# Two transformer blocks in one launch: the loads of the modulation weights and the first block's norms in another order

## What is computed

```python
cond = jax.nn.silu(c)                                   # c: (1, 1024)
mod = (cond @ ada_w[l] + ada_b[l])[:, None, :]          # ada_w: 1024 x 6144
sh1, sc1, g1, sh2, sc2, g2 = jnp.split(mod, 6, axis=-1)
h = rms_norm(x, ln1_g[l]) * (1.0 + sc1) + sh1
x = x + g1 * hybrid_mixer(h, w_in[l], w_out[l], ...)    # w_in: 1024 x 2840
h = rms_norm(x, ln2_g[l]) * (1.0 + sc2) + sh2
x = x + g2 * sparse_moe(h, ...)
```

## Time and profile before

| | |
|---|---|
| median of 3 runs | 2072.49 us (2072.33 to 2079.0) |
| the profiled execution, first to last instruction | 2071.6 us |
| PE busy | 1912.6 us (92%) |
| DVE busy | 498.4 us (24%) |
| ACT busy | 288.5 us (14%) |
| DMA | 547.34 MB, mean 264 GB/s |
| chain that ended last | PE 71%, DMA 22%, DVE 4%, ACT 2% |

### The profile page before, as it was taken

The page is one execution under the profiler, slowest core; times in us unless marked ns, Lnnn a source line. Parts: engine busy times, 40 slices in busy tenths (PEclk is TensorE's granted clock), DMA queues, the critical chain, the costliest instruction groups (busy, mean ns, idle before and its releaser), DMA issues.

```text
span 2071.6 us, 21989 instructions
## 1 busy us (share of the span) xinstructions
PE 1912.6 (92%) x8646; PEld 1104.0 (53%) x8647; DVE 498.4 (24%) x1026; ACT 288.5 (14%) x560; POOL 83.7 (4%) x115
## 2 busy tenths in 40 slices
PE   5987889999999999999999998989999989799997
PEld 2444733333333333333333335867788868678886
DVE  1236232212222222222212223132110015511001
ACT  1025101001110011001101101043110010311000
POOL 4003500000000000000000001000000001000000
PEclk9999889999999999999999999999999999899999
DMA  9682449969999999999999995311343433333430
GB/s 352 250 257 85 180 193 418 417 244 401 419 417 417 418 418 417 417 419 417 417 418 419 417 417 213 130 73 41 122 144 141 144 120 118 114 117 139 163 122 21
DMA packets 133761, 547.34 MB, mean 264 GB/s; under 512 B 5874, under 2 KB 9154, under 8 KB 97778
## 3 DMA queue, kind: packets, MB, share of 16 engines
q1 hardware_dynamic: 131536, 544.33, 66.8%
q10 hardware_dynamic: 2178, 2.34, 0.4%
HBM read 545.60 MB, written 1.05 MB: 264 GB/s over the span
## 4 chain that ended last, share of the span: by engine, by line
PE 71%; DMA 22%; DVE 4%; ACT 2%; issue 1%; SPq 0%; ACTq 0%; POOL 0%; DVEq 0%
PE ps L997 21%; DMA ring<-in_exp_w 20%; PE ps L949 14%; PE ps L1091 11%; PE ps L974 6%; PE ps L692 4%; PE ps L921 3%; PE ps L905 2%; PE ps L852 1%; PE ps L642 1%; DMA ring<-in_ada_w 1%; ACT arena L1145 1%; PE ps L1041 1%; PE ps L652 1%; PE ps L780 0%
## 5 line engine op out<-in xcount | busy, mean ns | idle before, releaser
L949 PE MATMUL ps<-ring,arena 128*64 128x512 f32 x2112 | 465.0, 595 | 13.7 <-DMA ring<-in_exp_w 13.7
L997 PE MATMUL ps<-hn,ring 128*128 128x272 f32 (+1 forms) x1792 | 415.4, 395 | 27.0 <-DVE hn L1679 16.0
L997 PEld LDWEIGHTS ps<-hn,ring 128*128 128x128 f32 x1792 | 346.0, 194 | 96.3 <-issue 23.4
L949 PEld LDWEIGHTS ps<-ring,arena 128*64 128x64 f32 x2112 | 155.8, 138 | 304.2 <-issue 266.8
L974 PE MATMUL ps<-arena 128*64 128x512 f32 x1056 | 233.9, 595 | 36.9 <-ACT arena L1145 36.9
L1091 PE MATMUL ps<-arena,ring 128*128 128x272 f32 (+1 forms) x1024 | 228.4, 386 | 1.0 <-ACT arena L1328 1.0
L1091 PEld LDWEIGHTS ps<-arena,ring 128*128 128x128 f32 x1024 | 194.4, 190 | 34.9 <-ACT arena L1328 1.8
L974 PEld LDWEIGHTS ps<-arena 128*64 128x64 f32 x1056 | 75.4, 137 | 174.2 <-issue 174.2
L1145 ACT ACTIVATE arena<-ps 128x512 f32<-128x512 f32 (+3 forms) x171 | 90.9, 536 | 373.4 <-PE ps L974 239.5
L921 PE MATMUL ps<-arena 128*128 128x512 f32 x272 | 132.4, 618 | 0.8 <-ACT arena L1145 0.8
L1626 DVE TENSOR_SCALAR arena<-arena 128x64 f32<-128x64 f32 x68 | 14.2, 251 | 391.4 <-PE ps L949 391.4
(11 more groups left out here) (341 smaller groups left out, 1201.9 us busy)
## 6 DMA issues: line engine op xcount, KB each, us to landing
ring<-in_exp_w SPq DMA_DIRECT2D x128, 2048.0 KB, 22.6
arena<-in_exp_w SPq DMA_DIRECT2D x64, 2048.0 KB, 19.6
ring<-in_mlp_w_up SPq DMA_DIRECT2D x16, 2048.0 KB, 7.6
ring<-in_mlp_w_down SPq DMA_DIRECT2D x16, 2048.0 KB, 7.7
ring<-in_ada_w SPq DMA_DIRECT2D x12, 2048.0 KB, 12.9
ring<-in_sb_w_qkv SPq DMA_DIRECT2D x6, 2048.0 KB, 14.4
ring<-in_w_in SPq DMA_DIRECT2D x5, 2048.0 KB, 9.9
ring<-in_lru_w_in SPq DMA_DIRECT2D x4, 2048.0 KB, 7.9
```

The lines of the kernel that those rows point to most:

```text
L949: last = mm(bank(2 + part)[64 * h:64 * h + 64, :], lhs, w[:, k % 2, at:at + 512], start=False, stop=(k == C - 1))
L997: last = mm(bank((n0 + q) % 8)[:, lo:TT], w[:, k, P * q:P * q + P], act[:, k, lo:TT], start=(k == 0), stop=(k == C - 1))
```

## The change

`A_LOADS` now brings group 0, all six chunks of `w_in`, the compressed layer's weights, and only then the eight loads of groups 1 and 2. SP no longer waits for the parameters. PE's modulation parts go from the projections to the compressed keys: group 1's four parts behind the hidden layer, group 2's four behind the compressed scores. `modulated_norm` is cut in three: `normed` (reciprocal and `x * rstd`), `affine`, and `modulated` (`* affine + shift` in one pass). For the first norm `normed` stands ahead of `modulation(0)`.

```diff
-A_LOADS = ([("ada", 0, k) for k in range(4)]
-           + [load for c in range(6) for load in (("in", 0, c), ("ada", 1 + c // 4, c % 4))]
-           + [("cmp", 0, 0), ("ada", 2, 2), ("ada", 2, 3)] + [("wout", 0, h) for h in range(2)])
+A_LOADS = ([("ada", 0, k) for k in range(4)] + [("in", 0, c) for c in range(6)] + [("cmp", 0, 0)]
+           + [("ada", 1 + k // 4, k % 4) for k in range(8)] + [("wout", 0, h) for h in range(2)])
...
-    sp.wait_ge(s["p0_loaded"], 16 * len(PARAMS[0]))
     for n, load_of in enumerate(A_LOADS):
...
         last.then_inc(s["z_done"], 1)
-        if t == 1:
-            if v == 1:
-                pe.wait_ge(s["root_ready"], 1)
-            modulation_part(1 + c // 4, c % 4)
...
     last.then_inc(s["cmp_hidden"], 1)
-    modulation_part(2, 2)
-    turn_modulation(1)
+    for k in range(4):
+        modulation_part(1, k)
     pe.wait_ge(s["cmp_gelu"], 1)
...
     last.then_inc(s["cmp_kv_done"], 1)
-    modulation_part(2, 3)
-    turn_modulation(2)
+    turn_modulation(1)
     pe.wait_ge(s["cmp_k_ready"], 1)
...
     last.then_inc(s["cmp_scored"], 1)
+    for k in range(4):
+        modulation_part(2, k)
+    turn_modulation(2)
...
-    def modulated_norm(number, gain, scale, shift):
-        link(v.scalar_tensor_tensor(m.affine[:], m.modT[:, scale:scale + C], 1.0, col(gain, C), ALU.add, ALU.mult))
+    def normed(number):
         dve.wait_ge(s["root_ready"], number)
         link(v.reciprocal(m.rstd[:, 0:T], m.root[:, 0:T]))
         first = chain.n
         for c in range(C):
-            v.scalar_tensor_tensor(m.hn[:, c, META:TT], m.xT[:, c, META:TT], m.affine[:, c:c + 1],
-                                   m.rstd[:, 0:T], ALU.mult, ALU.mult).then_inc(s["dve_chain"], 1)
+            v.tensor_tensor(m.hn[:, c, META:TT], m.xT[:, c, META:TT], m.rstd[:, 0:T],
+                            ALU.mult).then_inc(s["dve_chain"], 1)
         chain.n += C
+        return first
+    def affine(gain, scale):
+        link(v.scalar_tensor_tensor(m.affine[:], m.modT[:, scale:scale + C], 1.0, col(gain, C), ALU.add, ALU.mult))
+    def modulated(shift, first):
         for c in range(C):
             dve.wait_ge(s["dve_chain"], first + c + 1)
-            v.tensor_scalar(m.hn[:, c, META:TT], m.hn[:, c, META:TT], m.modT[:, shift + c:shift + c + 1],
-                            None, ALU.add).then_inc(s["h_ready"], 1)
+            v.tensor_scalar(m.hn[:, c, META:TT], m.hn[:, c, META:TT], m.affine[:, c:c + 1],
+                            m.modT[:, shift + c:shift + c + 1], ALU.mult, ALU.add).then_inc(s["h_ready"], 1)
...
-    modulation(0)
     dve.wait_ge(s["x_placed"], 4)
-    modulated_norm(1, PC_LN1, M_SC1, M_SH1)
+    made = normed(1)
+    modulation(0)
+    affine(PC_LN1, M_SC1)
+    modulated(M_SH1, made)
...
-    modulated_norm(2, PC_LN2, M_SC2, M_SH2)
+    affine(PC_LN2, M_SC2)
+    modulated(M_SH2, normed(2))
```

More of the change, by code:

```diff
@@ L1400, in modulated_norm @@
         for c in range(C):
-            v.scalar_tensor_tensor(m.hn[:, c, META:TT], m.xT[:, c, META:TT], m.affine[:, c:c + 1],
-                                   m.rstd[:, 0:T], ALU.mult, ALU.mult).then_inc(s["dve_chain"], 1)
+            v.tensor_tensor(m.hn[:, c, META:TT], m.xT[:, c, META:TT], m.rstd[:, 0:T],
+                            ALU.mult).then_inc(s["dve_chain"], 1)
         chain.n += C
+        return first
+    def affine(gain, scale):
+        link(v.scalar_tensor_tensor(m.affine[:], m.modT[:, scale:scale + C], 1.0, col(gain, C), ALU.add, ALU.mult))
+    def modulated(shift, first):
         for c in range(C):
             dve.wait_ge(s["dve_chain"], first + c + 1)
-            v.tensor_scalar(m.hn[:, c, META:TT], m.hn[:, c, META:TT], m.modT[:, shift + c:shift + c + 1],
-                            None, ALU.add).then_inc(s["h_ready"], 1)
+            v.tensor_scalar(m.hn[:, c, META:TT], m.hn[:, c, META:TT], m.affine[:, c:c + 1],
+                            m.modT[:, shift + c:shift + c + 1], ALU.mult, ALU.add).then_inc(s["h_ready"], 1)
+    dve.wait_ge(s["x_placed"], 4)
+    made = normed(1)
     modulation(0)
-    dve.wait_ge(s["x_placed"], 4)
-    modulated_norm(1, PC_LN1, M_SC1, M_SH1)
+    affine(PC_LN1, M_SC1)
+    modulated(M_SH1, made)
     dve.wait_ge(s["x_turned"], 5)
@@ L1472, in program_vector @@
     v.tensor_scalar(m.hid, m.hid2, 0.5, None, ALU.mult).then_inc(s["cmp_gelu"], 1)
-    modulation(1)
     dve.wait_ge(s["cmp_hidT_done"], 1)
@@ L1485, in program_vector @@
     v.tensor_copy(m.kcn[0:64, 0, :], m.kcn[0:64, 1, :]).then_inc(s["cmp_k_ready"], 1)
-    modulation(2)
+    modulation(1)
     dve.wait_ge(s["cmp_kT_done"], 1)
@@ L1511, in program_vector @@
                     ALU.mult).then_inc(s["cmp_probs"], 1)
+    modulation(2)
     for u in range(UNITS + 2):
```

## The result

| | before | after |
|---|---|---|
| median in the comparison (5 runs each) | 2076.01 us (2072.33 to 2079.0) | 2086.91 us (2082.97 to 2091.13) |
| ratio, 95% interval | 1 | 1.0055 (1.0038 to 1.0073) |
| the profiled execution | 2071.6 us | 2085.2 us |

The change makes the kernel slower by 0.55%. 3.5 of these are the kernel before itself, which ran at 2076.0 in the comparison and not at 2072.5; the other 11.8 are the change.

A forecast was written before the change was run, and what follows sets the result against it. It took a chain of waits to bound the kernel: group 0's loads, then PE up to attention. On the profiled span -6.0 - 3.05 - 10.4 + 19.6 - 0.8 - 0.2 = -0.9; median 2071.6 us, range 2066 to 2079.

The forecast's parts named there:

- The step that failed: At the start: ACT free at 12.1 us, before the parameters' turns, so its DMA issuing costs nothing; squares' sum ends at 24.3.
- the start: Up to the first projection matmul: without SP's wait and with the norm split, projections begin at 34.5 instead of 40.5, -6.0 us.
- The parameters: At the start: `x` shares DMA engines with group 0's loads and lands at 11.3, parameter set 0 at 14.5 us.
- The first rival: Start lost to its own transfers: parameters at about 20 us, projections at 40.5 and low clock; 2080.7 us, slower; 13%.
- The clock at the projections: First two projection half-chunks on PE run at 2.4 GHz after a shorter idle gap: -3.05 us (bounds -3.05 and 0).
- The parts: Projections on PE: six modulation parts of 1.85 us leave, five gained whole and 1.2 from the sixth: -10.4 us.
- The compressed keys: Hidden layer's end to attention: group 2's late loads land last, attention starts 32.2 us after instead of 12.6: +19.6 us.
- The fourth rival: Before attention: last loads land while small steps run, so they don't end last; attention at T + 20 (T: hidden layer's end), 2060 us; 4%.
- The attention's clock: Attention's first unit, held up about 1.6 us by the 1.2 GHz level; half of it gained, -0.8 us.
- The second norm: Second norm's products and adds on DVE: cheaper product, only first multiply-and-add ahead of the router matmuls: -0.2 us.
- Behind 277 us: From pass 0 to the end: the earlier difference is carried along whole, no further change.

The follow-up runs named there:

- the last experiment: Kernel before with the norm cut, `router_w` issued last of ACT's small loads and SP waiting only for `c`: 2068.4 us, 0.9968 of the kernel before.

## Why the prediction was wrong, point by point

**The step that failed** is "ACT was free at 12.1, before that, so its DMA issuing hides nothing and costs nothing", with its bound "if the longer backlog held its last two issues for up to 3 us". The issue behind `router_w` was held for 13.9 us, to 24.0, 7 past the parameters' landing. E, the end of the squares' sum, was 34.34 and not 24.3. Of these 10.0, 2.7 are the parameters (17.2 for 14.5), 6.75 the hold (E is 27.59 with `router_w` last; PE's sums took 5.85 in the kernel after and 5.52 in that one), 0.6 the rest. Another 0.9 came from the first `w_in` chunk, which landed E + 11.1 instead of E + 10.2, 9.12 after its issue (7.8). Sum 10.9, the whole miss at the start. The warning stood in the timeline of the kernel before, 0 to 25 us:

```profile
9.83 1.53 ACTq L1164 DMA_DIRECT2D rb<-in_router_b  x1
```

That is two to five times its neighbours' 0.3 to 0.7, at a moment when `x` had landed and group 0 had just begun. I had looked at when ACT was free and not at which issue had made it late.

**The parameters.** The sum was `x` alone 5.2, plus 16 packets in turn with q1's (4.7), plus 3.4. The turns came as said (626 packets to 621). What was missing is that `x` did not begin: from its issue at 1.44 to 5 us q1 moved 119 packets, seven an engine, and of `x` nothing. It landed at 13.84 instead of 11.3, and the parameters took the 3.4 behind it that I had given them. The later start in the last experiment takes this away.

**The first rival**, a start lost to its own transfers, was given 13% and 2080.7 us, and is nearest to what came. Its condition, parameters at about 20 us, did not hold (17.2), and neither did its price: with the parameters at 17.04 and ACT free, the projections start at 38.5, still 2 us before the old 40.51. Its direction was right and its mechanism is the smaller part. The rule behind it (the Trainium skill, "DMA: Bandwidth & Descriptors", section "Queues, rings and completion order": an engine drains a whole packet of some 9 to 17 descriptors before it turns to the next queue) is not what this case shows, and the measurement decides. In the earlier trace rows the 263 packets of q10 carry 0.03 MB, so each is one row of `router_w`; in the kernel after, from 20 to 24 us taken in tenths of a microsecond, the counts of the two queues never differ by more than 2, where turns of nine would differ by more. Only when group 0's loads ran out did q10 run ahead: 358 packets to 47 from 26 to 27 us. The rival's sum also had `x` landing alone, at 6.6, beside a full q1.

**The clock at the projections** (-3.05) came nearly: 2.3 to 2.6 less for the 192 records. The granted clock was 1.00 up to 46 us and 0.62 and 0.53 in the two windows of 2 us behind it. **The parts** (-10.4): -10.0 to -10.3. Right.

**The compressed keys** (+19.6): +21.1, near the upper bound of 22. The last load landed 29.85 behind the hidden layer (28.5 predicted) at 5.6 us a load instead of 5.0, and 7.45 for the first (8.4). Of the three waits of PE for `ada_w` two came, at 141.64 and 163.99; the middle one was covered by parts that ran partly at the low clock. But one reason given beside the sum was wrong: that the parts "cost nothing of their own" and that without late loads attention would start 18 to 20 us behind the hidden layer. Without them it starts at 30.25. The six parts that left the projections (11.1 us) come back here as PE's work. That leaves 6.6 of the 17.7 us that 30.25 is above the old 12.58. By estimate 2.1 are PE's wait for group 1's fourth load, which this version still has, and 4.3 are the clock: its scores take 3.62 (2.13 before) and its 64 part matmuls 9.87 (7.07 at 34.27 us in the kernel after). With group 2's loads it is 3.5 more, and a part of these is clock too (group 1's last part 3.31 in the kernel after, 1.92 without these loads). The fourth rival (4%, 2060) had therefore no such gain to give.

**The attention's clock** (-0.8) came to -0.1, but not because the first unit gave nothing. From its first matmul to L786, behind POOL's pass, it takes 7.76 us (9.36 before, to L790), so the 1.6 are gained in full. From there to the output projection it is 45.70 instead of 44.24: behind 3.56 us in which PE waits for POOL the granted clock falls again (0.77 and 0.80 from 174 to 182 us; 1.00 in the kernel before from 162 to 186). The low clock came one unit later. **The second norm** (-0.2) came to -0.4: one product of two tensors takes 418 ns (480 before), the multiply and add 406 (347 before), and the first kind is eight times on the chain, the second once.

**Behind 277 us** I had held the difference to be carried along. At pass 0 it is 11.3, at the end 13.6. The stretches of low clock lie elsewhere in the two executions. The chain of the kernel after, 1422 to 1436 us, and of the kernel before, 1410 to 1422 us, at the same unit of the second model's attention:

```profile
1428.20 1.18 PE ps L1037 x2
...
1430.53 1.63 PE ps L1037 x2
...
1432.92 0.90 ACT arena L1313
```

```profile
1415.94 0.99 PE ps L1041 x2
...
1417.53 0.82 PE ps L1041 x2
...
1418.98 0.90 ACT arena L1317
```

1.63 is twice 0.82: the same two matmuls at 1.2 instead of 2.4 GHz. From the first row to the ACT row there are 4.72 us here and 3.04 there. The executions of one kernel spread over 7 us (2071.54 to 2078.84 in 27 of the kernel before), and the clock goes with it: the mean granted clock was 0.978 in the fastest of them and 0.973 in the slowest. So spans of single executions are good to some 2 or 3 us only: the experiment that put SP's wait back expected 2077 and had 2076.3, though it lost 1.1 us more than expected in front of the attention. The medians say 10.9 for the change, the two spans 13.6.

**As a sum of its three edits**, from the profiled spans: taking SP's wait out costs 8.0 to 11.0 us (2073.3 against 2065.3, 2082.6 against 2071.6, and 8.9 in the kernel after, 2085.2 against 2076.3); the new order of loads and parts costs 11.9; the cut norm gains 6.3 in the kernel before and 9.3 where the wait is gone. 11.0 + 11.9 - 9.3 = 13.6, which closes by itself, since the four spans are taken in a row. The ratios to the kernel before are steadier and put the wait in the kernel after at some 7 (1.0055 against 1.0022) and the new order at some 9. The cut norm gives 6.3 at the end (5.8 by the medians, 2069.15 against 2074.91) when it gives 3.3 in its own two places. Another 1.8 appear between the router and pass 0 (272.26 - 241.98 against 277.37 - 245.31) and 1.2 behind, where it touches nothing. In the first of these the same pieces of PE in the two chains take other times, L905's eight records 1.95 against 2.79 and L893's 6.26 against 5.30, in sum 2.3 us less, so it is the clock there. Why the clock is kinder to this kernel (0.979 in the median of its executions, 0.975 in the kernel before) was not tested.

## What to carry to other kernels

Before a load is moved ahead, look at the other queues' DMA issues in the timeline and not only at when their engine is free: the one here that took several times its neighbours' time stood behind a load of many rows, and grew ninefold when traffic was added beside it. Issue the many-rowed load last; an engine with nothing to do would be another place for it, which no run here tried. Work that is taken out of one stage of a full engine and put into another is worth nothing by itself: ask first what the engine was waiting for in the new place, and where the answer is "nothing for as long as this takes", count it whole.

## What the runs showed of the hardware

- An issue of 128 bytes on ACT's queue took 13.74 to 14.04 us in four kernels behind a load of 1024 rows of 128 bytes with q1 full beside it; 1.33 to 1.77 where q1's loads had begun 2 to 3 us before it; 0.45 behind the same load with q1 idle and nothing older in ACT's queue; 0.29 ahead of the many-rowed load. The issue of the 1024 rows itself was over after 0.40 to 0.51 in every case. That the queue's room is what is lacking is inferred from this; no row shows its filling. It is not a fixed number of packets still to go: when the hold ended q10 had moved 800 to 805 of its 1986 packets in the four kernels, and 632 to 634 in the three with the wait.
- While both queues are full they take turns packet by packet, whatever the size: 261 of q1 (2.02 MB) to 263 of q10 (0.03 MB) from 15 to 20 us before, and within 2 of each other in every tenth of a microsecond from 20 to 24 us after. So 1024 rows of 128 bytes drain at the pace of as many 8 KB packets.
- 1.6 us in SP's first load (0.78 or 2.40) decide whether `x`, issued at 1.4, begins in its first two microseconds or only after 5 us: it took 12.4 us to land against 5.1, and the parameters came at 17.2 against 9.0. Why the late queue is passed over in the first microseconds is open.
- The low clock does not follow from the length of PE's gap alone: a modulation part of 1.92 us took 3.28 to 3.64 behind gaps of 2.2 to 3.3 us (three kernels), 2.44 behind 3.8 us in the last one, and 1.92 behind 2.1 us in the kernel without group 2's loads and behind 3.29 us in the kernel before.
